# A feed-forward output product with one more seven-product group in its second pass

## The reference

```python
def swiglu_ffn(x, w_in, w_out):
    gate, up = jnp.split(x @ w_in, 2, axis=-1)
    return (jax.nn.silu(gate) * up) @ w_out      # 256 x 5504 @ 5504 x 2048
...
x = x + 0.5 * swiglu_ffn(rmsnorm(x, ffn1_norm[l]), ffn1_w_in[l], ffn1_w_out[l])
h = rmsnorm(x, mix_norm[l])
proj = h @ w_in[l]
```

## Time and profile before

| | |
|---|---|
| median of 3 runs | 1767.77 us (1767.13 to 1771.47) |
| profiled execution: time, span | 1767.57 us, 1765.8 us |
| PE busy | 1759.7 us, 8052 matmuls |
| DVE busy | 1470.6 us |
| ACT busy | 1068.5 us |
| HBM traffic | 199 GB/s over the span |

### The profile page before, as it was taken

The page is one execution under the profiler, slowest core; times in us unless marked ns, Lnnn a source line. Parts: engine busy times, 40 slices in busy tenths (PEclk is TensorE's granted clock), DMA queues, the critical chain, the costliest instruction groups (busy, mean ns, idle before and its releaser), DMA issues.

```text
span 1765.8 us, 20884 instructions
## 1 busy us (share of the span) xinstructions
PE 1759.7 (100%) x8052; PEld 1468.4 (83%) x8052; DVE 1470.6 (83%) x1625; ACT 1068.5 (61%) x1357; POOL 29.0 (2%) x34
## 2 busy tenths in 40 slices
PE   9999999999999999999999999999999999999999
PEld 7888888888988888888888888888888888988887
DVE  7999999998899998575655655999999999899988
ACT  7666666666666666454545554666666666666564
POOL 0000000000000001100000000000000000000000
PEclk9999999999999999999999999999999999999999
DMA  9655555554645546555455457355555555554663
GB/s 375 229 214 212 199 190 191 191 191 156 249 168 217 222 169 230 185 184 183 155 187 167 167 168 261 126 208 192 210 213 213 213 214 186 199 192 158 238 219 103
DMA packets 156211, 350.84 MB, mean 199 GB/s; under 512 B 5992, under 2 KB 16256, under 8 KB 155984
## 3 DMA queue, kind: packets, MB, share of 16 engines
q1 hardware_dynamic: 153568, 341.88, 54.9%
q0 software_dynamic: 1424, 5.53, 1.0%
q10 hardware_dynamic: 1120, 2.10, 0.3%
HBM read 347.37 MB, written 3.69 MB: 199 GB/s over the span
## 4 chain that ended last, share of the span: by engine, by line
PE 99%; DMA 0%; DVE 0%; SPq 0%; ACT 0%; issue 0%
PE bank L545 10%; PE bank L546 10%; PE bank L547 10%; PE bank L529 7%; PE bank L531 7%; PE bank L530 7%; PE bank L486 7%; PE bank L488 7%; PE bank L487 7%; PE bank L617 6%; PE bank L618 6%; PE bank L616 6%; PE bank L643 2%; PE bank L644 2%; PE bank L642 2%; PE bank L514 1%
## 5 line engine op out<-in xcount | busy, mean ns | idle before, releaser
L1137 DVE TENSOR_TENSOR wlo<-raw,whi 128x1024 fp32r<-128x1024 f32 (+1 forms) x643 | 763.4, 1206 | 190.5 <-ACT whi L803 186.3
L803 ACT ACTIVATE whi<-raw 128x1024 fp32r<-128x1024 f32 (+1 forms) x643 | 668.5, 1046 | 408.4 <-PE bank L488 191.4
L545 PE MATMUL bank<-whi,xs 128*128 128x512 f32 (+1 forms) x768 | 298.5, 389 | 0.8 <-DVE wlo L1329 0.7
L547 PE MATMUL bank<-whi,xs 128*128 128x512 f32 (+1 forms) x768 | 296.2, 386 | 0.0
L546 PE MATMUL bank<-wlo,xs 128*128 128x512 f32 (+1 forms) x768 | 296.1, 386 | 0.0
L616 PE MATMUL bank<-whi,aw_hi 128*128 128x512 f32 x484 | 188.7, 390 | 0.0
L618 PE MATMUL bank<-whi,aw_lo 128*128 128x512 f32 x484 | 188.4, 389 | 0.0
L617 PE MATMUL bank<-wlo,aw_hi 128*128 128x512 f32 x484 | 188.3, 389 | 0.0
L545 PEld LDWEIGHTS bank<-whi,xs 128*128 128x128 f32 x768 | 144.7, 188 | 29.2 <-DVE wlo L1329 1.1
L547 PEld LDWEIGHTS bank<-whi,xs 128*128 128x128 f32 x768 | 144.7, 188 | 28.0
L546 PEld LDWEIGHTS bank<-wlo,xs 128*128 128x128 f32 x768 | 144.8, 189 | 26.8
(11 more groups left out here) (201 smaller groups left out, 2579.9 us busy)
## 6 DMA issues: line engine op xcount, KB each, us to landing
raw<-ffn_w_in SPq DMA_DIRECT2D x158, 1024.0 KB, 7.0
raw<-ffn_w_out SPq DMA_DIRECT2D x84, 1024.0 KB, 6.6
raw<-w_in SPq DMA_DIRECT2D x48, 1024.0 KB, 5.0
raw<-w_out SPq DMA_DIRECT2D x16, 1024.0 KB, 4.9
raw<-ffn_w_in SPq DMA_DIRECT2D x16, 768.0 KB, 4.9
x<-x SPq DMA_DIRECT2D x4, 512.0 KB, 11.7
raw<-ffn_w_out SPq DMA_DIRECT2D x4, 512.0 KB, 4.6
raw<-ffn_w_in SPq DMA_DIRECT2D x3, 512.0 KB, 8.2
```

Source lines behind the costliest of these rows:

```text
L545: mm(banks[b][:, 0:w], xs[:, k + i, 0, tok], hi, start=starts[b] and k + i == 0, stop=False, skip_group_check=True)
L547: last = mm(banks[b][:, 0:w], xs[:, k + i, 1, tok], hi, start=False, stop=k + i == last_k, skip_group_check=True)
L803: A(whi[:, h % SLOTS, 0:n_el], src, ACT.Copy).then_inc(weights_hi, 1)
L1137: V.tensor_tensor(wlo[:, h % SLOTS, 0:n_el], src, whi[:, h % SLOTS, 0:n_el].bitcast(f32), ALU.subtract).then_inc(weights_lo, 1)
```

## The change

- The second pass of each output product has four groups instead of three (16 tiles in groups, 27 plain), with leads 5, 2, 2, 2 instead of 6, 5, 5. It has 55 items instead of 52, and four behind the last T4 instead of six.
- The split sums of activations of the first three groups, made in the first pass, are kept for the second. `sfo` has room for four groups and lies in `xs`. The second pass makes them for the fourth group only.
- In the second pass the two activation splits of a group are made behind items T1 and B11, no longer both ahead of T1. PE waits for the first of them at B11 and for the second at B21.
- Group pieces go over `raw` slots 3, 4 and 5. The first piece of a group frees its slot when the T4 sum is made, the second when B22 is split. The T1 sum waits for the first piece alone, the T3 sum for the second.
- `x_turn(1, 0)` and `x_turn(1, 1)` stand behind the last two items, 53 and 54. The last two join steps come on DVE after all items.

```diff
-OUT_GROUPS = 3
-OUT_PLAIN = 4 * OUT_GROUPS
+OUT_GROUPS = (3, 4)
+OUT_PLAIN = [4 * g for g in OUT_GROUPS]
+KEPT = OUT_GROUPS[0]
-LEADS = ((8, 5, 5), (6, 5, 5))
+LEADS = ((8, 5, 5), (5, 2, 2, 2))
...
 def raw_slot(n):
-            q = OUT_LOADS[c][i] - 2 * OUT_GROUPS
-            return 3 + q % 2 if q < 0 else (c * ACT_PLAIN + q) % 3
+            q = OUT_LOADS[c][i] - 2 * OUT_GROUPS[c]
+            return 3 + (2 * c * OUT_GROUPS[0] + OUT_LOADS[c][i]) % 3 if q < 0 else (c * ACT_PLAIN[0] + q) % 3
...
-        place[0] = raw_at + 5 * 4 * W * 4
-        sfo = sb("sfo", [P, 4, 2, 2, P], f32r)
+        place[0] = xs_at
+        sfo = sb("sfo", [P, OUT_GROUPS[1] * 4, 2, 2, P], f32r)
+        def split_sums(g):
+            return sfo[:, 4 * g:4 * g + 4]
+        def kept(u, g):
+            return OUT_GROUPS[1] * u + g + 1
...
-                        item = ("form", q // 2, "T4") if q < 2 * OUT_GROUPS else ("plain", min(2 * q + 1, FT - 1))
+                        if q < 2 * OUT_GROUPS[c] and q % 2 == 0:
+                            return out_sums, 4 * group(u, c, q // 2) + 4
+                        item = ("form", q // 2, "B22") if q < 2 * OUT_GROUPS[c] else ("plain", min(2 * q + 1, FT - 1))
...
-                                pe.wait_ge(gs_ready, group(u, c, g) + 1)
+                                pe.wait_ge(gs_ready, kept(u, g))
-                            if f == "B11":
-                                pe.wait_ge(ga_ready, 2 * group(u, c, g) + 2)
+                            if f in ("B11", "B21"):
+                                pe.wait_ge(ga_ready, 2 * group(u, c, g) + (1 if f == "B11" else 2))
...
-                        if c and u == 0 and i in (OUT_LEN - 4, OUT_LEN - 2):
+                        if c and u == 0 and i >= OUT_LEN[1] - 2:
                             pe.wait_ge(p_joined, 8 + 4)
-                            x_turn(1, (i - OUT_LEN + 4) // 2)
+                            x_turn(1, i - OUT_LEN[1] + 2)
...
             def group_form_hi(u, c, g):
-                G = group(u, c, g)
-                if g or c:
-                    c0, g0 = (c, g - 1) if g else (c - 1, OUT_GROUPS - 1)
-                    act_e.wait_ge(weights_used, out_half(u, c0, ("form", g0, "B22")) + 1)
-                else:
-                    act_e.wait_ge(weights_lo, OUT[u])
-                act_e.wait_ge(gs_summed, 4 * G + 4)
-                A(sfo[:, :, :, 0, :], gs[c], ACT.Copy).then_inc(gs_hi, 1)
+                act_e.wait_ge(weights_used, OUT[u])
+                act_e.wait_ge(gs_summed, 4 * kept(u, g))
+                A(split_sums(g)[:, :, :, 0, :], gs[c], ACT.Copy).then_inc(gs_hi, 1)
...
+                            if c == 1 and f in ("T1", "B11"):
+                                group_act_hi(u, c, g, (0,) if f == "T1" else (1,))
...
                 if f == "T1":
                     full(n0)
-                    full(n1)
                     V.tensor_tensor(pair(tsum[:, 0:2 * W]), B12, B11, ALU.subtract).then_inc(out_sums, 1)
                 if f == "T3":
+                    full(n1)
...
-                                if d == 3:
-                                    group_form_sums(u, c1, g1)
-                                if d == 2:
-                                    group_form_lo(u, c1, g1)
+                                if d == 3 and c1 == 0:
+                                    group_form_sums(u, 0, g1)
+                                if d == 2 and c1 == 0:
+                                    group_form_lo(u, 0, g1)
+                                if d == 2 and c1 == 1 and g1 == KEPT - 2:
+                                    group_form_sums(u, 1, KEPT)
+                                if d == 2 and c1 == 1 and g1 == KEPT - 1:
+                                    group_form_lo(u, 1, KEPT)
...
+                        if c == 1 and item[0] == "form" and item[2] in ("T1", "B11"):
+                            group_act_lo(u, c, item[1], (0,) if item[2] == "T1" else (1,))
...
+                for step in range(OUT_LEN[1] - 1 - T4_ENDS[1], 6):
+                    join(u, 1, step)
```

More of the change, by code:

```diff
@@ L47 @@
 LOAD = {"B11": 0, "B12": 1, "B22": 2, "G0": 3, "B21": 4, "G1": 5, "U0": 6, "U1": 7}
-OUT_GROUPS = 3
-OUT_PLAIN = 4 * OUT_GROUPS
+OUT_GROUPS = (3, 4)
+OUT_PLAIN = [4 * g for g in OUT_GROUPS]
+KEPT = OUT_GROUPS[0]
 FORMS = ("T1", "B11", "T3", "T2", "B21", "B22", "T4")
-LEADS = ((8, 5, 5), (6, 5, 5))
+LEADS = ((8, 5, 5), (5, 2, 2, 2))
 def out_items(c):
-    items, plain = [], iter(range(OUT_PLAIN, FT))
-    for g in range(OUT_GROUPS):
+    items, plain = [], iter(range(OUT_PLAIN[c], FT))
+    for g in range(OUT_GROUPS[c]):
         items += [("plain", next(plain)) for _ in range(LEADS[c][g])]
@@ L69 @@
 OUT_ITEMS = [out_items(c) for c in range(PASSES)]
[L70 to L73, removed]
+OUT_LEN = [len(items) for items in OUT_ITEMS]
+OUT_AT = [0, OUT_LEN[0]]
+T4_ENDS = [OUT_ITEMS[c].index(("form", OUT_GROUPS[c] - 1, "T4")) for c in range(PASSES)]
+ACT_PLAIN = [ACT_PAIRS - 2 * g for g in OUT_GROUPS]
+PLAIN_TILES = [FT - k for k in OUT_PLAIN]
 def out_loads(c):
     at = {}
-    for g in range(OUT_GROUPS):
+    for g in range(OUT_GROUPS[c]):
         if g or c:
@@ L87, in out_loads @@
     loads = []
-    for i in range(ACT_PLAIN):
-        loads.append(2 * OUT_GROUPS + i)
+    for i in range(ACT_PLAIN[c]):
+        loads.append(2 * OUT_GROUPS[c] + i)
         for g in at.get(i, []):
@@ L99 @@
 OUT[0] = IN[0] + IN_LEN
-QKV = OUT[0] + PASSES * OUT_LEN
+QKV = OUT[0] + sum(OUT_LEN)
 WO = QKV + N_QKV * IN_HALVES
@@ L103 @@
 OUT[1] = IN[1] + IN_LEN
-END = OUT[1] + PASSES * OUT_LEN
+END = OUT[1] + sum(OUT_LEN)
 IN_P, OUT_P = [0, 0], [0, 0]
@@ L120, in out_half @@
 def out_half(u, c, item):
-    return OUT[u] + OUT_LEN * c + OUT_ITEMS[c].index(item)
+    return OUT[u] + OUT_AT[c] + OUT_ITEMS[c].index(item)
 def out_piece(u, c, q):
@@ L167, in layer @@
         x = sb("x", [P, TB, D_MODEL])
+        xs_at = place[0]
         xs = sb("xs", [P, KT, 2, SEQ], f32r)
@@ L643, in ffn_out @@
                                 mm(bank_out[:], st_hi, lo, start=False, stop=False, skip_group_check=True)
-                                last = mm(bank_out[:], st_lo, hi, start=False, stop=own and g == OUT_GROUPS - 1 and k == 1,
+                                last = mm(bank_out[:], st_lo, hi, start=False, stop=own and g == OUT_GROUPS[c] - 1 and k == 1,
                                           skip_group_check=True)
@@ L1203, in act_lo, with group_act_lo @@
                 V.tensor_tensor(aw_lo[:, a, a_in, :], act[:, k, :], aw_hi[:, a, a_in, :].bitcast(f32), ALU.subtract).then_inc(aw_ready, 1)
-            def group_act_lo(u, c, g):
-                for i in range(2):
+            def group_act_lo(u, c, g, part):
+                for i in part:
                     dve.wait_ge(ga_hi, 2 * group(u, c, g) + i + 1)
@@ L1211, in group_form_sums @@
             def group_form_sums(u, c, g):
-                G, t, S = group(u, c, g), 4 * g, gs[c]
+                G, t, S = kept(u, g) - 1, 4 * g, gs[c]
                 A11, A21, A12, A22 = act[:, t:t + 2, 0:P], act[:, t:t + 2, P:2 * P], act[:, t + 2:t + 4, 0:P], act[:, t + 2:t + 4, P:2 * P]
@@ L1217, in group_form_sums @@
                     dve.wait_ge(gs_ready, G)
-                if G and g == 0:
+                if u and g == 0:
                     dve.wait_ge(p_joined, 8 * PASSES * u)
@@ L1227, in group_form_lo @@
             def group_form_lo(u, c, g):
-                dve.wait_ge(gs_hi, group(u, c, g) + 1)
-                V.tensor_tensor(sfo[:, :, :, 1, :], gs[c], sfo[:, :, :, 0, :].bitcast(f32), ALU.subtract).then_inc(gs_ready, 1)
+                dve.wait_ge(gs_hi, kept(u, g))
+                V.tensor_tensor(split_sums(g)[:, :, :, 1, :], gs[c], split_sums(g)[:, :, :, 0, :].bitcast(f32), ALU.subtract).then_inc(gs_ready, 1)
             def out_sum(u, c, g, f):
@@ L1261, in join @@
                     dve.wait_ge(p1_copied, PASSES * u + c + 1)
-                    dve.wait_ge(gs_ready, group(u, c, OUT_GROUPS - 1) + 1)
+                    dve.wait_ge(gs_ready, kept(u, OUT_GROUPS[c] - 1))
                     V.tensor_tensor(u2, P6[:], p1s[:], ALU.add).then_inc(p_joined, 1)
```

62 lines of the change are left out of this document (32 added, 30 removed).

## The result

| | median | lowest to highest | runs |
|---|---|---|---|
| before | 1767.08 us | 1766.41 to 1771.47 | 11 |
| after | 1772.26 us | 1771.41 to 1774.66 | 11 |

The ratio is 1.0029 [1.0021, 1.0037]: 5.2 us slower. The forecast was 1768.9, its range ended at 1771.3. The prediction had put what can be told at 5.3 us; the interval is narrower and lies wholly above 1, and so the 5.2 us are a real loss, though a small one. The profiled execution took 1771.86 us.

The account below looks back on a forecast made before the run. PE's way through its matmuls, 0.227 us between starts, was taken as the bound, DVE close behind; - 2.7 + 3.7 + 0.2 = + 1.2 us on the profiled 1767.57, runs' median 0.2 higher: 1768.9 us, range 1764.8 to 1771.3.

Parts of the forecast that it names:

- The saving, by distance: Second passes: 12 matmuls fewer at 0.227 us between starts, 2.7 us saved; by busy time 4.7.
- The passes: Inside the passes: DVE's added and moved sums and splits stay covered by its lead over PE, so cost nothing.
- The rival with the third group's first piece late: In both passes a late load holds up DVE and PE; 1774 us and more, chance 0.09.
- First, half 0 of the projections: At the projections' start PE wants half 0's split 0.4 us before DVE ends it.
- Second, the chain of `x_turn(1, 2)`: Third transpose of x: ACT and DVE take 6.3 us from `whi` of half 2; 1.0 us late without a DMA wait.
- Third, the weights: Projections' loads: half 2's piece waits for the copies into `dmat`; `x_turn(1, 2)` 3.7 us late, the first 0.4 included.
- t + 7.3: Forecast landing of half 2's weights, in us from t, the start of `x_turn(1, 0)` on PE.
- My own upper end, t + 9: Latest landing allowed for half 2's weights, from the start of `x_turn(1, 0)`; hand-over cost then 5.5 us.
- The 97.5%: Share of the DMA engines the copies into `dmat` had at 686 to 687 us before; taken as holding up the weights.
- my rival: Copies and weights' queue have half the engines each; cost 2.4, 1767.5 us; chance 0.25, shared with copies not mattering.
- the clock: TensorE at 1.2 GHz behind the third transpose of x: forecast 0.
- The end of the kernel: Last three items, bank by bank: PE waits 0.2 us for the last `aw_lo`.

Follow-up runs that it names:

- experiment 9: 7 with three groups in the second pass (leads 6, 5, 5) instead of four; 1767.46 us against 1767.39 for the kernel before, ratio 1.0000.
- 7: Changed kernel with projections slots 0, 1, 2, first two transposes of x one item earlier, leads 4, 2, 2, 2; 1764.65 us against 1767.24 before, ratio 0.9983.
- experiment 2: Changed kernel with the projections' pieces in raw slots 0, 1, 2 instead of 2, 0, 1; 1766.69 us against 1767.31 before, ratio 0.9996.
- experiment 1: Changed kernel with POOL issuing the copies into `dmat` six halves later; 1766.42 us against 1767.31 before, ratio 0.9995.
- 5: Kernel before with the projections' pieces in raw slots 1, 2, 0, the first in the last item's slot; 1773.84 us against 1767.24 before, ratio 1.0032.
- 8: Changed kernel with the projections' third load held back until half 0 is split; 1772.04 us against 1767.39 before, ratio 1.0028.
- experiment 4: Changed kernel with eight matmuls, results unread, in PE's stop ahead of the third transpose of x; 1771.46 us against 1767.31 before, ratio 1.002.
- experiment 3: Changed kernel with the third and fourth transposes of x one half of the projections later; 1768.19 us against 1767.31 before, ratio 1.0003.
- experiment 6: Changed kernel with projections slots 0, 1, 2 and the first two transposes of x one item earlier; 1764.96 us against 1767.24 before, ratio 0.9984.

## Why the prediction was wrong, step by step

- **The saving, by distance: right.** 2.7 us; experiment 9 against 7 shows 2.70, with the end's 0.36 added. The busy time would have said 4.7.
- **The passes: right.** I costed the added sums and splits at nothing, with leads of 0.8 and 1.1 left at the second and third groups. Weight splits on DVE and the items that use them on PE:

```profile
611.21 1.22 DVE L1149 TENSOR_TENSOR wlo<-raw,whi 128x1024 fp32r<-128x1024 f32 x1
...
613.18 0.39 PE L629 MATMUL bank<-whi,aw_hi 128*128 128x512 f32 x1
...
634.00 1.22 DVE L1149 TENSOR_TENSOR wlo<-raw,whi 128x1024 fp32r<-128x1024 f32 x1
...
636.30 0.39 PE L629 MATMUL bank<-whi,aw_hi 128*128 128x512 f32 x1
```

  611.21 + 1.22 to 613.18 is 0.75, 634.00 + 1.22 to 636.30 is 1.08. The rival with the third group's first piece late didn't occur either: PE has no wait in the second passes.
- **First, half 0 of the projections: right, 0.2 short.** 0.6 for 0.4.
- **Second, the chain of `x_turn(1, 2)`: right.** 6.27 for 6.3. That it costs about 1 us without a wait for the load, half 0 included, is what experiment 2 shows: 0.6 for half 0 and 0.6 beyond it (6.08 for 5.45), 1.2 for 1.0. In experiment 1 the second part is 1.1 (6.54), with 0.7 us of waiting for the load still in it.
- **Third, the weights: this step failed, in its size.** I wrote that the 1 MB "ends about 2.6 us later, at t + 7.3". I had divided bytes by the queue's rate, as if all 16 engines ended together, and taken that for the landing. Fifteen engines were through by t + 7.85; ACT may start only at the sixteenth, t + 9.0. My own upper end, t + 9, was read from a landing, which has such a lag in it (692.43 and 693.41 for its fifteenth and sixteenth update), and it held: 5.5 late against 5.4 measured (4.8 + 0.6). This is 1.7 of the 4.0 us by which the sum was off.
- **The 97.5% was read wrongly too, without harm to this number.** I took it that the copies "have the engines". On SP's timeline of before, one load is issued at 680.24 and the next only at 685.79:

```profile
680.24 0.37 SPq L354 DMA_DIRECT2D raw<-w_in  x1
...
685.79 0.37 SPq L354 DMA_DIRECT2D raw<-w_in  x1
```

  and the queues from 685 to 686 us, one window ahead of the earlier trace rows, were

```profile
q0 software_dynamic: 72, 0.29, 72.1%
q1 hardware_dynamic: 63, 0.10, 27.5%
```

  nearly packet for packet, 72 and 63, of which 12 have 4 bytes. From 686 to 687 us the last bytes of the load of 680.24 passed, and that of 685.79 had not begun. The copies had the engines because nothing else was there to move. From 687 to 688 us the load of 685.79 should have been:

```profile
q1 hardware_dynamic: 1, 0.00, 0.1%
```

  Its first bytes came at 688.89, 3.1 us behind its issue. Loads issued to an empty queue with no copies running had them 1.0 us behind (678.74 to 679.78 after, 697.60 to 698.63 before). Why this one began so late, with the copies running, no run shows; so for those 2 us "the copies have the engines" was what the trace had. The result does not depend on it, for after the change the loads were under way before the copies' first bytes. The rule that I set aside, in the Trainium skill (DMA: Bandwidth & Descriptors, Queues, rings and completion order), that an engine goes round its queues packet by packet, is what the trace of after shows: 343 packets to 339. It gives halves in packets and not, as my rival had it, in bytes. The second load ends behind the copies in either case, all bytes of both have to pass first, and so it ends at the same time. That the term came out near t + 7.3 by a wrong share is therefore no merit of the working. A load that ends before the copies would have been forecast far too late.
- **What was not in the prediction: the clock. This term failed as well; it was put at nothing without a reason.** I priced a wait of PE at its length. A wait of 4.6 us cost 2.2 more, since TensorE came out of it at 1.2 GHz. This is the larger half of the error, and it put the result over the range's end: with it my upper end of 1770.7 would have been 1772.9.
- **The end of the kernel: right, 0.2 short.** 0.4 for 0.2: `aw_lo` ends at 1757.36 + 0.41, PE's step over it is 0.47 for 0.23, and from L677 to the last matmul there are 8.11 us for 7.93. The rows answer to the earlier trace rows.

```profile
1757.36 0.41 DVE L1215 TENSOR_TENSOR aw_lo<-act,aw_hi 128x256 fp32r<-128x256 f32 x1
...
1757.36 0.39 PE L631 MATMUL bank<-whi,aw_lo 128*128 128x512 f32 x1
1757.83 0.50 PE L677 MATMUL bank<-whi,aw_hi 128*128 128x512 f32 x1
```

Shown by the runs: that the loads' landing makes the stop (1, 2, 5), that the copies delay the landing (1) and the third load doesn't (8), what the fourth groups save (9), and what the fallen clock costs (the table in 4). The clock fell with stops of 4.2 to 4.6 us (after, 5, 8) and in 4, where PE stood still for 2.2 us and then ran the eight; it stayed full with stops of 0.4 to 1.5 (1, 2, 3).

Shown by the traces, but by no run made for it: that the lag of 1.6 to 1.9 us between the bytes and the landing is for the most part, 1.1 to 1.4 us, one engine's. It does not hang on the copies (1) nor on the third load (8). In the kernel after and in experiments 1, 5 and 8 the last load ahead of the 16 KB instruction packet has no such lag, and the next one has it. That the packet is its cause fits, but was not tested, and it can't be the only one: in experiment 6 a load's last updates are 1.3 us apart (683.72 and 684.99) when the packet comes at 684.87.

## What to carry to other kernels

When a change shifts which item of a stage ends last, look up which buffer that item holds, whether the next stage's first load wants the same one, and what else the same semaphore sets free; here one constant in a slot formula was worth 6 us (1305.80 to 1299.41). A queue's share of the engines in a window does not say by itself who has precedence: look whether the other queue had bytes to move. Take the time to a landing from landings, not from bytes over bandwidth, since one engine that is behind holds up the whole load. And price a single long stop of PE at more than its length: here stops of 4.2 to 4.6 us cost 1.4 to 2.2 us more.

## What the runs showed of the hardware that I had not expected

- Behind 4.6 us without work TensorE's granted clock was 0.50 (1.2 GHz) for 4.5 us, at a cost of 2.2 us. In experiment 4 it was still full after 2.2 us without work and fell during the eight matmuls that followed; after 1.5 us (experiment 3) it stayed full. Stops of 4.2 and 4.5 us (experiments 5 and 8) cost 1.4 and 1.7 more. In each case the cost was half the time in which PE worked at 0.50.
- Two DMA queues shared the engines packet for packet, and so 0.27 to 0.14 MB in a microsecond, since their packets were 4 and 2 KB (kernel after, 684 to 689 us).
- A load's landing was seen 1.6 to 1.9 us behind the time at which its queue had moved as many bytes. Fifteen of its sixteen semaphore updates were there 1.1 to 1.4 us earlier than the last (690.40 and 691.53 after, 689.25 and 690.61 in experiment 1).
